# Two transformer-like blocks in one kernel: residual layers and value projections with tokens on partitions, and a token-major residual stream

## What is computed

```python
# first block
z = rms_norm(x, mix_norm_g) @ w_in            # in1: mq mk mv mo, gates, fq fk fv
ha, hb = mlstm(...), forgetting_attention(...)
x = x + concat(ha, hb) @ w_out                # out1
a, g = split(rms_norm(x, ffn_norm_g) @ w_up)  # up1
x = x + (gelu(dwconv(a)) * g) @ w_down        # down1
gate = sigmoid(rms_norm(x, ple_norm_g) @ w_ple_gate)
x = x + gate * (p @ w_ple_proj)               # gate1, proj1
# second block; sh, sc, g come from silu(c) @ w_mod + b_mod
h = rmsnorm(x, mix_pre_w) * (1 + sc_m) + sh_m
y = hybrid_mixer(h, w_in, ..., w_out)         # in2, out2
x = x + g_m * rmsnorm(y, mix_post_w)
h = rmsnorm(x, ffn_pre_w) * (1 + sc_f) + sh_f
y = conv_ffn(h, w_up, conv_w, w_down)         # up2, down2
x = x + g_f * rmsnorm(y, ffn_post_w)
```

## Time and profile before

| | |
|---|---|
| runs | 2607.34, 2609.37, 2611.34 us; median 2609.37 |
| profiled execution, first to last instruction (span) | 2606.0 us |
| its mean granted TensorE clock | 0.985 |
| TensorE busy | 2533.7 us (97%), 14987 matmuls |
| TensorE weight loads | 2229.2 us (86%) |
| VectorE busy | 1886.1 us (72%) |
| ScalarE busy | 1190.1 us (46%) |
| GpSimd busy | 242.6 us (9%) |
| DMA | 545.71 MB, mean 209 GB/s |
| chain that ended last | PE 95%, DVE 3%, ACT 1% |

### The profile page before, as it was taken

The page is one execution under the profiler, slowest core; times in us unless marked ns, Lnnn a source line. Parts: engine busy times, 40 slices in busy tenths (PEclk is TensorE's granted clock), DMA queues, the critical chain, the costliest instruction groups (busy, mean ns, idle before and its releaser), DMA issues.

```text
span 2606.0 us, 40350 instructions
## 1 busy us (share of the span) xinstructions
PE 2533.7 (97%) x14987; PEld 2229.2 (86%) x14987; DVE 1886.1 (72%) x2480; ACT 1190.1 (46%) x1247; POOL 242.6 (9%) x430
## 2 busy tenths in 40 slices
PE   7999999899999999999997999998999999999997
PEld 6888888788888888889987888887788888888897
DVE  4777577688888887666788667765777777776665
ACT  5444445344444444444454445455444444444443
POOL 1111000012121221111140000000000000001110
PEclk9999999999999999999998999999999999999998
DMA  6667555578888887777765555554466666667774
GB/s 201 218 203 220 151 154 167 165 252 275 269 279 270 277 270 258 250 250 243 267 224 161 170 156 159 172 191 147 139 184 184 190 185 187 185 186 265 250 244 154
DMA packets 261953, 545.71 MB, mean 209 GB/s; under 512 B 20097, under 2 KB 21121, under 8 KB 261841
## 3 DMA queue, kind: packets, MB, share of 16 engines
q1 hardware_dynamic: 230497, 442.91, 54.2%
q0 software_dynamic: 31040, 100.98, 11.3%
q10 hardware_dynamic: 304, 0.27, 0.0%
HBM read 541.98 MB, written 2.10 MB: 209 GB/s over the span
## 4 chain that ended last, share of the span: by engine, by line
PE 95%; DVE 3%; ACT 1%; issue 0%; POOL 0%; ACTq 0%; POOLq 0%; DVEq 0%
PE PS L1620 55%; PE PS L1624 30%; PE PS L1617 5%; PE PS L1639 1%; PE PS L1944 1%; PE PS L1661 0%; DVE mix L1068 0%; DVE xT L1520 0%; PE PS L1655 0%; DVE mix L1047 0%; PE PS L1791 0%; DVE w_lo L949 0%; PE PS L1675 0%; PE PS L1689 0%; PE PS L1690 0%
## 5 line engine op out<-in xcount | busy, mean ns | idle before, releaser
L1620 PE MATMUL PS<-xs,w_hi 128*128 128x512 f32 x4864 | 1733.4, 401 | 30.0 <-DVE xs L1062 18.1
L526 ACT ACTIVATE w_hi<-w_raw 128x1024 fp32r<-128x1024 f32 x832 | 879.7, 1059 | 1142.7 <-PE PS L1624 1105.8
L949 DVE TENSOR_TENSOR w_lo<-w_raw,w_hi 128x1024 fp32r<-128x1024 f32 x832 | 1015.3, 1224 | 527.8 <-ACT w_hi L526 512.6
L1624 PE MATMUL PS<-xs,w_lo 128*128 128x256 f32 x4992 | 1393.2, 282 | 0.0
L1620 PEld LDWEIGHTS PS<-xs,w_hi 128*128 128x128 f32 x4864 | 915.6, 189 | 252.5 <-issue 32.5
L1624 PEld LDWEIGHTS PS<-xs,w_lo 128*128 128x128 f32 x4992 | 949.3, 190 | 6.9
L475 POOL DMA_DIRECT2D mod_w<-in_w_mod x384 | 207.6, 541 | 2325.8 <-DVE hs L1290 914.3
L1624 PE MATMUL PS<-hs,w_lo 128*128 128x256 f32 x1408 | 394.5, 281 | 0.0
L1620 PE MATMUL PS<-hs,w_hi 128*128 128x512 f32 x1056 | 372.2, 397 | 0.0
L936 DVE SCALAR_TENSOR_TENSOR mod_acc<-mod_w,c_act,mod_acc 128x512 f32<-128x512 f32 x360 | 269.0, 747 | 19.6 <-DMA mod_w<-in_w_mod 11.2
L1624 PEld LDWEIGHTS PS<-hs,w_lo 128*128 128x128 f32 x1408 | 266.9, 190 | 0.6
(11 more groups left out here) (298 smaller groups left out, 1375.7 us busy)
## 6 DMA issues: line engine op xcount, KB each, us to landing
w_raw<-in_w_up SPq DMA_DIRECT2D x352, 512.0 KB, 4.5
w_raw<-in_w_in SPq DMA_DIRECT2D x208, 512.0 KB, 3.9
mod_w<-in_w_mod POOLq DMA_DIRECT2D x384, 256.0 KB, 4.6
w_raw<-in_w_down SPq DMA_DIRECT2D x176, 512.0 KB, 4.5
w_raw<-in_w_out SPq DMA_DIRECT2D x64, 512.0 KB, 4.0
w_raw<-in_w_ple_gate SPq DMA_DIRECT2D x32, 512.0 KB, 4.4
mix<-in_x SPq DMA_DIRECT2D x4, 512.0 KB, 5.9
w_raw<-in_w_ple_proj SPq DMA_DIRECT2D x4, 512.0 KB, 6.7
```

Of the source, the lines that this page charges most:

```text
L526: nc.scalar.activation(w_hi[:, slot, :, :], w_raw[:, slot, :, :], ACT.Copy).then_inc(hi_made, 1)
L949: V.tensor_tensor(w_lo[:, slot, :, :], w_raw[:, slot, :, :], w_hi[:, slot, :, :].bitcast(F32), ALU.subtract).then_inc(lo_made, 1)
L1620: return M(PS[:, bank + b, :], w_hi[:, slot, k, b * P:(b + 1) * P], x(c), start=start, stop=stop)
L1624: return M(PS[:, bank + b, 0:T], w_lo[:, slot, k, b * P:(b + 1) * P], x(c)[:, 0:T], start=False, stop=False)
```

## The change

The residual stream becomes `xr`, tokens on partitions (two tiles of 128 tokens by 2048 channels). Layers, or strips of them, that are marked `rows` in the layer table are multiplied the other way round: a block of `hi` or `lo` tokens is stationary and 512 weights of the strip move, into two banks for the two token tiles. They are the strips 0, 3, 6, 9 of in1b and 2, 3 of in2 (values), and all of out1, down1, the gate, proj, out2 and down2. There is no `half` and no joined strip in them. proj is cut in two, proj1a behind gate1a and proj1b behind gate1b.

A token's sum of squares is now one ScalarE operation along a row with `accum_out`, into a column of `stat`; root and reciprocal work on two columns. The rows are scaled by VectorE into `xn` and transposed by TensorE (L1737) for the next layer's operand, gains and shifts being applied on the way out of PSUM. The gate's operand is transposed strip by strip in down1 (L1745). The post-norm gains of out2 and down2, which are now needed along the row, are spread over the partitions by matmuls with a diagonal (`spread`, `copy_gain`). In the last strip of out1, proj1b, out2 and down2 (`halves`) the first token tile's end is signalled before the second's. In out1, proj1b and out2 the weight split for the group four after the last (`late`) is moved behind the first chunks of the norm. The 16 modulation tiles of a strip of down1 and down2 are spread over 6 groups.

```diff
-        "out1": Layer(2, g16, unrolled=True, residual=True, joined=True),
...
+        "in1a": Layer(1, g16, unrolled=True),
+        "in1b": Layer(6, g16, unrolled=True, mod=0, mod_pairs=3, rows=(0, 3, 6, 9)),
+        "out1": Layer(2, g16, unrolled=True, rows="all", late=True),
+        "down1": Layer(2, g44, unrolled=True, mod=14, mod_per_pair=2, rows="all"),
+        "gate1a": Layer(1, g16, unrolled=True, mod=18, rows="all"),
+        "proj1a": Layer(1, 1, unrolled=True, rows="all"),
+        "gate1b": Layer(1, g16, unrolled=True, rows="all"),
+        "proj1b": Layer(1, 1, unrolled=True, rows="all", late=True),
+        "in2": Layer(6, g16, unrolled=True, mod=19, mod_pairs=1, rows=(2, 3)),
+        "out2": Layer(2, g16, unrolled=True, rows="all", late=True),
+        "down2": Layer(2, g44, unrolled=True, mod=20, mod_per_pair=2, rows="all"),
...
-        first, groups = g16, layer.G - 4 - g16
+        first, groups = g16, layer.G - 8 - g16
...
-        return s if j == layer.G - 2 else None
+        return s if j == layer.G - 6 else None
...
+            def row_squares(m, k, out=square_out):
+                for t in range(2):
+                    ins = nc.scalar.activation(out[:, t, :], xr[:, t, strip_cols(k)], ACT.Square, accum_out=part(m, t, k))
+                ins.then_inc(S["row_sq"], 1)
...
-                nc.scalar.activation(xT[:, NB * k:NB * k + NB, :], x_turned(k), ACT.Copy).then_inc(S["x_copied"], 1)
...
+            def norm_hi(name, gain, shift=None, after=None):
...
+                    wait("xn_turned")
...
+                            ins = nc.scalar.activation(xs[:, c, 0:T], turned[:, b, :], ACT.Identity, scale=gain[:, c:c + 1],
+                                                       bias=shift[:, c:c + 1])
...
+            def to_rows(layer, i, s, ps):
+                k = 2 * i + s
+                x = xr[:, :, strip_cols(k)]
+                if k < 3 or not layer.late:
+                    strip_used(layer, i, s)
+                    V.tensor_tensor(x, x, ps[:, 0:2, :], ALU.add).then_inc(evac_done, 1)
+                    return
+                wait("row_half")
+                V.tensor_tensor(x[:, 0, :], x[:, 0, :], ps[:, 0, :], ALU.add).then_inc(S["row_added"], 1)
+                strip_used(layer, i, s)
+                V.tensor_tensor(x[:, 1, :], x[:, 1, :], ps[:, 1, :], ALU.add).then_inc(evac_done, 1)
...
+                def scale(c, n):
+                    for t in range(2):
+                        ins = V.tensor_scalar(xn[:, t, c * P:(c + n) * P], xr[:, t, c * P:(c + n) * P], rstd_of(m, t), None, ALU.mult)
+                    ins.then_inc(S["xn_made"], 1)
+                def lo(q, c0, n):
...
+                        ins = V.scalar_tensor_tensor(xs[:, c, T:2 * T], turned[:, b, :], gain[:, c:c + 1], less, ALU.mult, ALU.subtract)
+                    ins.then_inc(S["x_ready"], 1)
+                for q, n in enumerate(NORM_CHUNKS):
+                    scale(firsts[q], n)
+                    if q >= 2:
+                        lo(q - 2, firsts[q - 2], NORM_CHUNKS[q - 2])
+                    if q == 3:
+                        late_lo(after)
...
+            def add_post(m, z, made):
+                rstd(m)
+                for k in range(4):
+                    c = strip_cols(k)
+                    for t in range(2):
+                        ins = V.scalar_tensor_tensor(xr[:, t, c], z[:, t, c], rstd_of(m, t), xr[:, t, c], ALU.mult, ALU.add)
+                    ins.then_inc(S[made], 1)
...
+                            if layer.in_rows(i, s):
+                                for t in range(2):
+                                    for k in range(GK):
...
+                                        x_hi, x_lo = (x(c)[:, e * T + t * P:e * T + (t + 1) * P] for e in range(2))
+                                        o = PS[:, bank + t, :]
...
+                                        M(o, x_hi, w_hi[:, slot, k, :], start=begin, stop=False)
+                                        M(o, x_hi, w_lo[:, slot, k, :], start=False, stop=False)
+                                        ins = M(o, x_lo, w_hi[:, slot, k, :], start=False, stop=end)
+                                    if halves and t == 0 and layer.last(i, s, j):
+                                        ins.then_inc(S["row_half"], 1)
```

More of the change, by code:

```diff
@@ L64, with __init__ @@
     count_h = 0
[L66 to L69, removed]
+    def __init__(self, pairs, groups, unrolled=False, mod=None, mod_per_pair=1, mod_first=0, mod_pairs=None, rows=(),
+                 late=False):
+        self.pairs, self.G, self.unrolled, self.late = pairs, groups, unrolled, late
+        self.rows = range(2 * pairs) if rows == "all" else rows
         self.mod, self.mod_per_pair, self.mod_first = mod, mod_per_pair, mod_first
@@ L1399, in gla_decay @@
+            stream("gate1a", None, side=gate1a_side)
+            stream("proj1a", to_embed(0))
+            stream("gate1b", None, side=gate1b_side)
+            stream("proj1b", to_embed(2))
+            wait("row_sq", 5)
+            whole_mean(MIX2, 4)
+            rstd(MIX2)
+            norm_rows("in2", scale_m, shift_m, after="proj1b")
             def gla_decay(h):
@@ L1534, in _, with out2_side @@
-            rstd()
-            norm_apply(scale_f, shift_f)
+            def out2_side(n, j):
+                if j == 1:
+                    diag_gain(gate_m, n)
+            stream("out2", to_post(POST2, z1), side=out2_side)
+            dve.wait_ge(evac_done, 2 + layers["out2"].end)
+            add_post(POST2, z1, "mixed")
+            wait("row_sq", 4)
+            whole_mean(FFN2, 4)
+            rstd(FFN2)
+            norm_rows("up2", scale_f, shift_f, after="out2")
             def up2_piece(layer, i, s, j):
@@ L1584, in all_out, with stream @@
                 pe.wait_ge(evac_done, 2 + layers[name].end)
-            def stream(name, x, ready=None, first=0, chunks=(4, 4, 4, 4), side=None):
+            def stream(name, x, ready=None, first=0, chunks=(4, 4, 4, 4), side=None, norm=False, halves=False):
                 layer = layers[name]
@@ L1881, in _, with after_up, down1_side @@
-            stream("down1", blocks_of(hs), side=down_side("down1", "up1"))
+            stream("out1", lambda c: xf[:, c - FOX_OUT, :] if c >= FOX_OUT else xs[:, c, :], ready=4, first=FOX_OUT, side=mixers1_end, halves=True)
+            stream("up1", blocks_of(xs), ready=8, chunks=NORM_CHUNKS, norm=True)
+            def after_up(up, n, j):
+                if n == 0 and GK * (j + 1) == FB - NB:
+                    pe.wait_ge(evac_done, 2 + layers[up].end)
+            def down1_side(n, j):
+                after_up("up1", n, j)
+                if n and j == 3:
+                    pe.wait_ge(evac_done, layers["down1"].n0 + n + 2)
+                    if n > 1:
+                        pe.wait_ge(S["x_ready"], 13 + n - 1)
+                    turn_strip("down1", n, n - 1)
@@ L1911, in _ @@
-            stream("gate1b", blocks_of(xs), side=gate1b_side)
-            strip_sum(spare("gate1b", 1) + 2)
-            wait("ss_read")
+            stream("proj1a", blocks_of(ps_in))
+            stream("gate1b", blocks_of(xs))
+            stream("proj1b", blocks_of(ps_in), halves=True)
             def mixers2(n, j):
```

756 lines of the change are left out of this document (355 added, 401 removed).

## The result

The change makes the kernel slower: 2627.8 us (median of 4 runs, 2626.7 to 2628.6) against 2609.2 us for the kernel before beside it, a ratio of 1.0075 with a 95% interval of 1.0062 to 1.0087. The forecast was 2554 us and its range ended at 2580. In what follows each kernel's time stands as its ratio to the kernel before on the same chip; a difference between two kernels is the difference of their ratios times 2607 us, certain to about 5 us.

What follows compares the result with a forecast made beforehand. TensorE, busy 97% of 2606.0 us, was taken as the bound, through its matmul groups and four seams. Seven gains sum to 55.6 us, giving 2550.4, plus 3.4 for the median: 2554 us, range 2525 to 2580.

Steps and rivals of the forecast that it cites:

- Step 8: Mod tiles in down1 and down2: 6 groups for 16 tiles suffice, 13.8 us needed of 16.6; priced at nothing.
- Rival D: Mod tiles land too slowly, stalling TensorE in each of 8 strips; 2619 us if landing takes 11 us; chance 0.03.
- Steps 4 and 5's last remark: After seams into in2 and up2, VectorE's 16.7 us before group four's split just fits; 2 us may be lost at each.
- Rival C: Seams give half back: late first weight splits stall up1, in2, up2 by 2 to 4 us each; 2566 us, chance 0.12.
- step 2: Small work in TensorE's stream: transposes and summing passes out, 148 passes of 0.11 us in; net 2.3 us gained.
- step 7: The start: four copies of x go, VectorE waits less before the first matmul; 2.5 us gained (0 to 4).
- Step 1: Residual layers: twelve 512-column matmuls replace 16 or 24 in 324 groups, 2.77 us a group; 19.0 us gained.
- Rival B: A matmul's fixed part shows fully: pitch 2.70 us, step 1 gives 42 us, 2531 us in all; chance 0.13.
- Rival A: TensorE is paced by columns alone: a new group takes 2.82 us, step 1 gives 4 us; 2570 us, chance 0.22.
- The rule cited in the prediction: A warm matmul costs columns over 2.4 plus 2.5 ns; by it step 1 would be some 5 us, not 19.
- Steps 3 to 6: Seams out1 to up1, into in2, out2 to up2, and the end: 4.4, 6.0, 11.4 and 10.0 us gained.
- Step 3: Seam out1 to up1: the rewritten norm chain takes 5.5 us against 9.96, 4.4 us gained.

Runs made afterwards that it cites:

- a5_down1_late_sum: Changed kernel with down1's mod sum moved back to two groups before the strip's end, its 16 tiles still put into 6 groups; ratio 1.0032 to the kernel before.
- d1_chunks_early: Changed kernel with weight splits of groups four and five and the last chunk's transposes earlier in up1, in2, up2; ratio 0.9999 to the kernel before.
- e1_down1_channels: Kernel with all mends, but down1's 88 groups multiplied in the old weight-stationary form on TensorE; ratio 0.9804 to the kernel before.
- c2_all: Changed kernel with mod tiles respaced (not down2's strip 0), gains spread later, chunks and two splits earlier, start's norm earlier; 2543.9 us, ratio 0.9758 to the kernel before.

## Why the prediction was wrong

**Step 8 failed, and it decides the sign.** "Priced at nothing; the cover is the ring." The sum divided the landing time by four: 4.6 / 4, 12 tiles in 13.8 us with 16.6 to spend. What a ring of four gives is a round, which is landing, the consumer's turn, and the way to the next issue: some 6.0 us, so 12 tiles need 17.9, more than the 16.6, and it became 22.5 with VectorE's weight splits (1.22 us each) between them. Both added terms stood in the trace of before, the 0.75 us in the earlier trace rows, and the way to the next issue in the timelines of VectorE and GpSimd, where an addition ends at 1251.29 and the issue that it releases starts 0.65 us later:

```profile
1250.55 0.74 DVE L936 SCALAR_TENSOR_TENSOR mod_acc<-mod_w,c_act,mod_acc 128x512 f32<-128x512 f32 x1
1251.94 0.54 POOL L475 DMA_DIRECT2D mod_w<-in_w_mod  x1 [1.49 <-DVE mod_acc L936]
```

The working also took VectorE's time and the tiles' time apart, but in one in-order queue a wait for a tile delays the next weight split (`a5_down1_late_sum`), so the lag was not 2.6 us. The price: 25 us in down1, 19 in three strips of down2, and one strip more, which at the same rate makes 50 us (an estimate). Without them the changed kernel would be at about 2578 us, faster than the kernel before.

**Rival D** was the right place, kind of wait and side, at 3 in 100. Its working would not have found the size: it let only the landing time grow (8.3 us before anything is lost), and that did not grow at all. And each stop was priced at its idle time, without the half clock behind it: 3.07 us of idle cost 6.3, and 3.02 cost 4.9.

**Steps 4 and 5's last remark**, "it just fits; 2 us may be lost at each": 6.0 us were lost in in2 and in up2 each, and 4.5 in up1, of which the remark does not speak; with the slow stretches behind them the three came to 20 us (`d1_chunks_early`). The prediction summed VectorE's work (16.7 us in 14 to 15) and took the work as the limit; it was idle for 5 us of it. The limit was an order: transposes before group four's matmuls on TensorE, the split behind the chunk on the others. The order of instructions on three engines, read side by side, shows such a ring; a sum of busy times doesn't. Rival C names this stop, at half its size, and puts it down to VectorE's late split of weights.

**Stops that no step had**: the gains' spread, 11 us, counted in step 2 as 64 passes of 0.11 us and not as 8 hand-overs from VectorE; and the first norm's spread, a stop of 4.9 us whose mend was worth some 3, not clear of noise. It outweighs what step 7 gained, 1.8 us of the 2.5 forecast (the first matmul came 0.9 us earlier, the second stop shrank by 0.9).

**Step 1** was right in kind and too small: 0.045 and 0.11 us a group were 0.095 and 0.16 (with the 2.815 and 2.88 that the prediction put for the old forms), so 256 x 0.095 + 68 x 0.16 = 35 us where 19 were forecast. Rival B had it (2.70 us). The single pair of the earlier trace rows, 0.225, was the better evidence than its neighbours' average. Rival A, columns alone, is refuted: 2.72, 2.83 and 2.88 us for the same 6144 columns, and `e1_down1_channels`. The rule cited in the prediction, from the Trainium skill, "TensorE: Matmul & The Clock Gate", section "Back-to-back issue gap", is given there for a matmul by itself, and would have made this form 2.59 us; no run shows a steady pitch under 2.72.

**Steps 3 to 6** hold: 3.6, 4.8, 12.0 and 10.3 us gained for 4.4, 6.0, 11.4 and 10.0. (Step 3's terms come to 5.4 us before the hand-overs that it adds, so its 5.5 has room for only one of them; 6.3 was measured.)

The account closes: 2606.0 - 35 - 2.3 - 30.6 - 1.8 = 2536 us would be the span without new stops. The changed kernel's span lies 90 us above that, and that of `c2_all`, 2544.6, 9 us above it: one stop of 4.4 us at a mod sum is left in it, and one of 1.8 at the start. Step 2's 2.3 us was not measured by itself, and the 35 us of step 1 rest on pitches; only down1's part of them was measured apart (`e1_down1_channels`).

## What to carry to other kernels

A ring of N buffers delivers N items per round, and a round is landing time plus the consumer's turn plus the time until the next load is issued; hold that against the deadline before tiles are pushed together. Where a queue is in order, ask of each wait what stands behind it and whether the awaited engine is itself waiting for that: busy sums say "it fits" of a ring of waits. And a stop of 3 us in TensorE's stream cost 1.6 to 2 times its length here, since the half clock behind it counts too.

## What the runs showed of the hardware

At a granted clock of 1.00 a matmul, each with its own weights, cost its columns at 2.4 GHz and 13 to 14 ns: 12 of 512 columns took 2.72 us, over some 200 groups, and 24 of 256 columns 2.88, over some 50 groups of the kernel before. The same 16 mixed matmuls take 2.77, 2.83 or, in the other order, 2.81 us; what sets which was not found. Behind a stop of 3.07 us TensorE's granted clock was 0.50 for 5.3 us and more. A tile of 256 KB landed 4.6 us after the start of its issue, and the ring of four, with four tiles loaded before, gave 16 in 22.5 us. The mean clock of the span was 0.985 before, 0.978 after, 0.990 with the mends, though TensorE's busy share was 97% and 96% in the first two.
